# Block inverse of the delta rule: corrections computed for half of the columns

## The reference, cut to what matters

```python
lmat = jnp.where(strict, jnp.einsum('nbhik,nbhjk->nbhij', kb, k) * decay, 0.0)
amat = lmat + jnp.eye(C, dtype=jnp.float32)
rhs = jnp.concatenate([v * beta[..., None], kb * jnp.exp(gc)[..., None]], axis=-1)
sol = lax.linalg.triangular_solve(amat, rhs, left_side=True, lower=True, unit_diagonal=True)
```

## Time and profile before

| quantity | value |
| --- | --- |
| median of three runs | 1752.03 us (1749.71 to 1754.26) |
| profiled execution, own time | 1760.79 us |
| span of its trace | 1759.0 us |
| mean granted TensorE clock | 0.966 |
| PE busy | 1667.0 us, 95% of the span |
| DVE busy | 765.3 us, 44% |
| first round of the inverse, levels 2 to 32 | 328.9 to 354.5 us from the span's start |
| second round, levels 2 to 32 | 374.1 to 413.2 us |
| recurrence alone | 418.9 to 435.0 us |

### The profile page before, as it was taken

One profiled execution on the slowest core, in us unless ns is written; L12 is line 12 of the kernel. 1 busy time (PEld: TensorE's weight loads), 2 busy tenths in 40 slices (PEclk: granted clock), 3 DMA queues, 4 the chain that ended last, 5 costly groups with the idle time before them and its releaser, 6 DMA issues.

```text
span 1759.0 us, 31567 instructions
## 1 busy us (share of the span) xinstructions
PE 1667.0 (95%) x13326; PEld 1568.5 (89%) x13326; DVE 765.3 (44%) x1403; ACT 607.2 (35%) x1120; POOL 531.3 (30%) x187
## 2 busy tenths in 40 slices
PE   6999888999988999999999999989889999999998
PEld 6999756888887899999999997559878999999998
DVE  4119753443574632222223623784746322223235
ACT  4113373221443442222223314783434323222232
POOL 4533300210252133443433432002621443433441
PEclk9999998899999999999999998899999999999999
DMA  5232300000433023223222223001320223222221
GB/s 150 74 95 76 119 26 1 8 2 13 144 114 103 25 72 97 82 87 96 89 78 95 73 96 133 1 1 49 120 97 25 80 89 97 90 78 95 81 86 51
DMA packets 123034, 131.39 MB, mean 75 GB/s; under 512 B 6285, under 2 KB 115122, under 8 KB 122930
## 3 DMA queue, kind: packets, MB, share of 16 engines
q1 hardware_dynamic: 116064, 123.27, 21.5%
q10 hardware_dynamic: 6866, 6.63, 1.2%
HBM read 122.44 MB, written 7.45 MB: 74 GB/s over the span
## 4 chain that ended last, share of the span: by engine, by line
PE 84%; DVE 10%; ACT 3%; issue 2%; DMA 0%; ACTq 0%; DVEq 0%
PE LP L722 66%; PE MP L839 3%; PE LP L1044 3%; PE LP L805 3%; PE MP L823 2%; DVE acc L1790 1%; DVE sq L2014 1%; PE LP L957 1%; DVE sq L2012 1%; DVE xl L1797 1%; PE MP L1138 1%; DVE probs L1856 1%; PE MP L1124 1%; PE MP L1132 0%; DMA stage<-in_w_in_ab 0%
## 5 line engine op out<-in xcount | busy, mean ns | idle before, releaser
L619 POOL TENSOR_TENSOR wl<-stage,wh 128x2048 fp32r<-128x2048 f32 x107 | 493.5, 4612 | 1017.5 <-ACT wh L1294 1017.4
L722 PE MATMUL LP<-xh,wh 128*128 128x272 f32 x2176 | 458.3, 292 | 14.3 <-DVE xl L1797 7.2
L722 PE MATMUL LP<-xh,wl 128*128 128x272 f32 x2176 | 452.9, 290 | 0.0
L722 PE MATMUL LP<-xl,wh 128*128 128x272 f32 x2176 | 452.3, 290 | 0.0
L1294 ACT CAST wh<-stage 128x2048 fp32r<-128x2048 f32 x107 | 203.7, 1904 | 462.7 <-PE LP L722 461.9
L722 PEld LDWEIGHTS LP<-xh,wh 128*128 128x128 f32 x2176 | 345.6, 190 | 19.3 <-DVE xl L1797 9.7
L722 PEld LDWEIGHTS LP<-xl,wh 128*128 128x128 f32 x2176 | 345.7, 191 | 0.0
L722 PEld LDWEIGHTS LP<-xh,wl 128*128 128x128 f32 x2176 | 342.9, 190 | 0.0
L722 PE MATMUL LP<-hh,wh 128*128 128x272 f32 x1024 | 211.2, 287 | 0.0
L722 PE MATMUL LP<-hh,wl 128*128 128x272 f32 x1024 | 210.6, 288 | 0.0
L722 PE MATMUL LP<-hl,wh 128*128 128x272 f32 x1024 | 210.3, 287 | 0.0
(11 more groups left out here) (357 smaller groups left out, 1877.7 us busy)
## 6 DMA issues: line engine op xcount, KB each, us to landing
stage<-in_w_up SPq DMA_DIRECT2D x32, 1024.0 KB, 5.3
stage<-in_w_down SPq DMA_DIRECT2D x32, 1024.0 KB, 5.2
stage<-in_w_in_ab SPq DMA_DIRECT2D x13, 1024.0 KB, 5.2
stage<-in_w_xkv SPq DMA_DIRECT2D x8, 1024.0 KB, 5.4
stage<-in_w_in_c SPq DMA_DIRECT2D x6, 1024.0 KB, 5.0
stage<-in_w_out_ab SPq DMA_DIRECT2D x4, 1024.0 KB, 7.1
stage<-in_w_xq SPq DMA_DIRECT2D x4, 1024.0 KB, 5.6
stage<-in_w_xo SPq DMA_DIRECT2D x4, 1024.0 KB, 5.9
```

The source lines that it names most:

```text
L619: pool.tensor_tensor(wl[s][:, :], stage[s][:, :], wh[s][:, :].bitcast(f32), ALU.subtract).then_inc(w_lo, 1)
L722: mm = pe.matmul(LP[:, 2 * slot + half, 0:b - a], weights, X[part][:, k, a:b], start=(first and n_ == 0), stop=(last and n_ == 2), skip_gr ...
```

## The change

A level joins blocks of size n in pairs. The correction of `Tm` is nonzero only in the first n columns of every 2n, that of `TmT` only in the second n. `half_of` selects these columns: a strided view with runs of n elements. The moving operands of `dt` and `dtt` become 32 columns for a chunk instead of 64 (16 instead of 32 for the sample), the products go packed into the first half of the region that they used, and VectorE subtracts these from the strided half of `Tm` or `TmT`. The number of instructions and their order, weights, semaphores and the steps `x`, `uw` and all others are as before.

```diff
+        def half_of(m, n, second):
+            axes = "p h (b r c) -> p h b r c" if len(m.shape) == 3 else "p (b r c) -> p b r c"
+            pairs = m.rearrange(axes, r=2, c=n)
+            return pairs[:, :, :, second, :] if len(m.shape) == 3 else pairs[:, :, second, :]
...
                     if k < len(sizes) - 1:
                         for h, p in each():
-                            mm = mm_(b0[p, w + h * C:w + h * C + C], TmT[s][p, h, :], Xm[s][p, h, :])
+                            out = b0[p, w + h * C // 2:w + (h + 1) * C // 2].rearrange("p (b c) -> p b c", c=sizes[k])
+                            mm = mm_(out, TmT[s][p, h, :], half_of(Xm[s][p, h, :], sizes[k], 0))
                         mm.then_inc(inv_pe[s], 1)
                     for h, p in each():
-                        mm = mm_(b1[p, h * C:h * C + C], Xm[s][p, h, :], TmT[s][p, h, :])
+                        out = b1[p, h * C // 2:(h + 1) * C // 2].rearrange("p (b c) -> p b c", c=sizes[k])
+                        mm = mm_(out, Xm[s][p, h, :], half_of(TmT[s][p, h, :], sizes[k], 1))
                     mm.then_inc(inv_pe[s], 1)
...
+                    def halves(bank, at):
+                        return bank[0:P, at:at + w // 2].rearrange("p (h b c) -> p h b c", h=H, c=sizes[k])
...
-                            dve.tensor_tensor(TmT_, TmT_, heads(b1, 0), ALU.subtract).then_inc(inv_dve[s], 1)
+                            second = half_of(TmT_, sizes[k], 1)
+                            dve.tensor_tensor(second, second, halves(b1, 0), ALU.subtract).then_inc(inv_dve[s], 1)
...
-                            dve.tensor_tensor(T_, T_, heads(b0, w), ALU.subtract).then_inc(inv_dve[s], 1)
+                            first = half_of(T_, sizes[k], 0)
+                            dve.tensor_tensor(first, first, halves(b0, w), ALU.subtract).then_inc(inv_dve[s], 1)
```

## The result

The changed kernel takes 1802.75 us in the median of 4 runs (1800.42 to 1805.24), against 1753.14 us (4 runs) before: a ratio of 1.0253, 95% interval 1.0210 to 1.0295. The changed kernel is slower, far outside the range given. The mean granted clock of its four runs is 0.936 to 0.939; the profiled execution before had 0.966.

What follows compares the result with a forecast made beforehand. TensorE, busy 95% of the span, was taken to bound the kernel. Gains of 0.4 us there and 0.3 us from VectorE took 1752.0 us to 1751.3 us, no change; the 8-in-10 range was 1745.5 to 1761 us.

Steps and rivals of the forecast that it cites:

- What bounds the stage: Delta rule: the chain runs block to block on TensorE, 7.62 us a second-round level; the distance between records counts.
- The halved columns on TensorE: Products dt and dtt: weight loads keep their distance when fewer columns move; 0.4 us gained in sum.
- two tails of 0.027: Last pass of a block before another tile shape: 0.027 us saved at each of 12 places, 0.32 us.
- Rival 1: Products dt and dtt: moved columns set the distance, so 17.0 us halve, 8.5 us less, 1743.2 us; 11%.
- Rival 3: Moved operand of dt and dtt: short runs read slowly, 10.8 us more at full price, 1762 us; 4%.
- One reading on the way: Sample's loads of 32 columns (8 in 0.32 us): closer together than the prompt tiles', so distance shrinks when both sides shrink.
- VectorE: 36 subtractions from TmT and Tm: 0.42 to 0.28 us each, 5.0 us less work, almost all hidden.
- The part on the path: Level 32, where uw waits 0.20 us for TmT: 0.14 us goes in each round, 0.3 us.
- sum of 0.7 us: Whole kernel: 0.4 us on TensorE plus 0.3 us of VectorE gained; no change forecast, 70%.
- Rival 2: Delta-rule levels: the clock falls, 2.9 us per fall of 6.8 us; three falls give 1760.1 us; 15% for two or more.
- Its dearest case: Clock rival's extreme: whole second round at the low clock, 29.7 us more, 1781 us.
- The failed argument: Recurrence, 418.9 to 435.0 us: keeps clock 1.00 with half-wide blocks and waits for VectorE, so speaks against a fall.

Runs made afterwards that it cites:

- e1: Changed kernel, but TensorE moves all 64 columns in strided order and VectorE still subtracts half; 1755.57 us against 1755.62, ratio 1.0001.
- e2: Kernel before with halved products and subtractions only in the second round; 1770.89 us, ratio 1.0067; its profiled execution took 1750.0 us.
- e8: Kernel before with one unread product of 512 columns, three of 256, and merged running-sum products keeping the program's length; 1751.53 us, ratio 0.9966.
- e3: Kernel before with halved products and subtractions only in the first round; 1773.02 us, ratio 1.0086.
- e4: Changed kernel with only dt halved, in products and subtractions, and dtt at all columns; 1781.12 us, ratio 1.0110.
- e5: Changed kernel plus one unread product of 512 columns after each level of the second round; 1790.89 us, ratio 1.0171.
- e6: Changed kernel plus five unread products of 512 columns in one burst after the second round's last level; 1819.53 us, ratio 1.0349.
- e10: Changed kernel with the fillers and merged running-sum product of e8; 1786.60 us, ratio 1.0181.
- e11: Changed kernel with only dtt halved, in products and subtractions, and dt at all columns; 1760.44 us, ratio 1.0035.
- e9: Kernel before plus six unread products of 64 columns (24 records) in the wait after the delta rule; 1779.20 us, ratio 1.0128.
- e7: Kernel before plus unread products in TensorE's waits: two of 512 columns before the first round, four of 256 in the recurrence; 1769.67 us, 1.0052.

## Why the prediction was wrong

**What bounds the stage: right.** TensorE, block after block, in both rounds and in both kernels.

**The halved columns on TensorE: right.** In the stretch of the first round at full clock, the weight loads of the changed kernel stand as far apart as before; a timeline (start us, us, engine, line, operation, shape, count):

```profile
333.79 0.55 PEld L1050 LDWEIGHTS LP<-TmT,Xm 64*64 64x64 f32 x16
333.82 0.63 PE L1050 MATMUL LP<-TmT,Xm 64*64 64x32 f32 x16
```

0.55 us for 16 loads, as in the earlier trace rows. At 1.00 a block of 32 is 1.05 us instead of 1.08, and a level 0.05 us shorter: two tails of 0.027. Rival 1 is refuted: of 17.0 us nothing but the tails goes. Rival 3 too: e1, with all columns in the order of the short runs, is as fast as the kernel before. One reading on the way holds only in part: the sample's loads are closer together than those of the prompt's tiles if two of the latter, side by side, count as one (0.040 against 0.069 us); by single records they are not (0.040 against 0.034).

**VectorE: right.** Groups by shape in the changed kernel (count, busy us, mean ns), to be held against the earlier trace rows:

```profile
L2101 DVE TENSOR_TENSOR TmT<-TmT,LP 128x128 f32<-128x128 f32 x20 | 5.7, 287 | 11.4 <-PE LP L1050 11.2
...
L2107 DVE TENSOR_TENSOR Tm<-Tm,LP 128x128 f32<-128x128 f32 x16 | 4.5, 284 | 14.2 <-PE LP L1050 14.2
```

0.287 and 0.284 us, where 0.28 was taken; 4.9 us less work. At the end of the second round the chain of e2, at full clock, goes from the levels into `uw` without a piece of VectorE:

```profile
402.12 2.76 PE LP L1050 x53
```

Before, the first load of `uw` waited 0.20 us there. The part on the path is gone as said.

**The clock: the step that failed.** The sum of 0.7 us has no term for the clock: it takes the second round and the recurrence as staying at 1.00. This is the term that was put at nothing; in the profiles the stretch from `d2` of the second round to the next projection grew by 41.9 us. Rival 2 had the mechanism and the side, at 15%, and its price was mis-sized: "Three, which I take as its time, give 8.8" us. The trace has one fall of 102 us, from 375.1 to 477.5. Its price per microsecond was good: 1.76 was used and a level took 13.59 / 7.57 = 1.80 times as long. Its dearest case, the whole second round for 29.7 us, still ended the fall ahead of `uw` and the recurrence. The failed argument is the one against a long fall: "the recurrence alone, 418.9 to 435.0, keeps 1.00". It does when it starts at 1.00. The changed kernel's recurrence starts at 0.50, does the same work, and stays at 0.50. Nor does it "consist" of half-wide blocks: `qs` and `o` move 64 columns, `ws` and `ds` 128. To keep the clock and to get it back are two different things, and only the first was in the earlier trace rows. The question to ask was the other one: what TensorE did where the clock came back, at 334.1 and at 368.2 us, and whether that work is still there after the change. At 368.2 it was in the products of the step `gram` (up to 256 moved columns), which are not touched. But at 334.1 it was in the corrections of the first round's level 2, which the change halves. In the second round, too, `d2` was such a place: with all columns e8 left its low stretch there within 3.4 us. The first round's level 2 in the kernel before (start us, us, engine, line, operation, shape, count):

```profile
333.21 1.05 PE L1044 MATMUL LP<-TmT,Xm 64*64 64x64 f32 x16
334.06 0.66 PE L1044 MATMUL LP<-Xm,TmT 64*64 64x64 f32 x16
```

The forecast's range took low stretches of the length seen before (6.8 us) as given. But the length isn't fixed: with all columns a fall at `d2` lasted 3.4 us (e3, e8), with halved ones 27 us or more (the changed kernel, e4, e5, e6, e10; the 27 in e5, with its wide products).

**What is open.** Shown is that the loss is low clock and that it comes with the moved columns taken away: all columns give the old time (e1), and wide products lift the clock (e5, e6). The profiles suggest that the halved columns keep it from coming back soon, rather than that they bring it down. Not shown is what starts the fall at the second round's beginning, where none of that round's halved products has run; the profiles of the changed kernel, e4, e5, e6 and e10 have it there and so have e3 and e8, with all columns in that round, while the kernel before, e1, e2 and e11 passed without it in the executions profiled. Nor why halving in the first round alone costs 15 us (1.0086), or why `dt` alone seems to cost more than `dtt`. These differences are between shares of executions that fall, and single profiles don't explain them.

## What to carry to other kernels

Halving the moved columns of an fp32 product whose weights are as wide as it saved next to nothing here (0.05 us a level), because the weight loads already stand at that distance, and it takes away streaming on which the clock may depend. Before narrowing a matmul in a stretch that is bound by TensorE, look for the granted clock around it: if it falls and recovers near there, the work that recovers it may have value beyond its result. Single long executions among those of before (here 1766 to 1781 us beside 1753) may be a sign of such a stretch.

## What the runs showed that was not expected

What is granted seems to depend on what was granted before: the recurrence alone ran 16 us at 1.00 in the kernel before and 28.8 us at 0.50 in the changed one, with the same instructions, and with TensorE busy for all of its time in the second case and waiting for VectorE in the first. Being busy without gaps at the low clock didn't lift it; one product of 512 columns per level did, after 27 us. The Trainium skill (TensorE: Matmul & The Clock Gate, section What's actually happening) has activity release the throttled state. That e5's and e6's wide products lifted the clock agrees; that TensorE was busy for 57.10 of 57.10 us at 0.50 doesn't, if to be active is to be busy, and here the measurement decides.

24 more records in TensorE's program ahead of a loop cost 17 us inside that loop, 11.3 us of it (11.6 in e9) in four waits for nothing that the profile names and the rest in low clock around them (e7), with 95 instead of 77 fetches on the instruction queue. The Trainium skill (Runtime: NRT & Kernel Launch, section Instruction fetch mechanics) says that instructions are fetched in blocks of 256 and that a taken branch out of the held blocks stalls until its target is fetched; the fetches and waits of e7 and e9 agree, though no run here shows how many blocks the loop spans. An experiment that adds instructions needs a control of the same length.
